# Stick-breaking sums over later keys: fp32r products of a high and a low part in place of fp32 products

## The reference

```
z = einsum('bhqd,bhkd->bhqk', q, k) / sqrt(64)
causal = key_pos < t
log_keep = where(causal, log_sigmoid(-z), 0)
tail = cumsum(log_keep, axis=keys, reverse=True)
between = concatenate([tail[..., 1:], 0])
weights = where(causal, exp(log_sigmoid(z) + between), 0)
out = einsum('bhqk,bhkd->bhqd', weights, v)
...
y = concatenate([y_dilated, y_lru, y_stick * silu(gate)])
x = x + y @ w_out
```

## Time and profile before

| | |
|---|---|
| median of 3 runs | 1189.01 us (1188.92 to 1189.37) |
| profiled execution | 1189.2 us, span 1187.4 us |
| granted TensorE clock | 0.998 of full |
| busy | TensorE 98%, its weight loads 88%, VectorE 62%, ScalarE 48%, GpSimd 2% |
| HBM | 177 GB/s over the span |

### The profile page before, as it was taken

How to read it: one execution, slowest core, us unless ns; L and a number is a source line. 1 busy time by engine, 2 the same in 40 slices (tenths; PEclk the granted TensorE clock), 3 DMA queues, 4 the chain that set the end, 5 groups by cost and what they waited for, 6 DMA issues and landing times.

```text
span 1187.4 us, 18024 instructions
## 1 busy us (share of the span) xinstructions
PE 1164.1 (98%) x7560; PEld 1041.3 (88%) x7560; DVE 737.5 (62%) x982; ACT 570.6 (48%) x656; POOL 25.9 (2%) x35
## 2 busy tenths in 40 slices
PE   6999999999999999999999999999999899999997
PEld 5978998998999988888998898899988689978995
DVE  4866655668555456685755657755554667775674
ACT  5454445534444434444444534445432466855673
POOL 0000000001000000000000000000000100000000
PEclk9999999999999999999999999999999999999999
DMA  8744545555765554644545457565556353437320
GB/s 293 261 168 156 174 146 177 188 194 169 265 191 186 175 197 141 237 153 142 177 142 192 163 194 230 195 211 183 194 196 213 124 193 128 141 128 253 130 84 35
DMA packets 129823, 211.44 MB, mean 178 GB/s; under 512 B 6480, under 2 KB 52560, under 8 KB 129616
## 3 DMA queue, kind: packets, MB, share of 16 engines
q1 hardware_dynamic: 126944, 202.96, 50.9%
q0 software_dynamic: 1744, 6.29, 1.9%
q10 hardware_dynamic: 1056, 1.05, 0.3%
HBM read 209.24 MB, written 1.05 MB: 177 GB/s over the span
## 4 chain that ended last, share of the span: by engine, by line
PE 93%; DVE 3%; ACT 3%; issue 1%; DMA 0%; POOL 0%; DVEq 0%; POOLq 0%; ACTq 0%
PE ps L432 89%; PE ps L621 1%; ACT wh L895 1%; PE ps L656 1%; PE ps L756 0%; DMA hml<-in_xT 0%; PE ps L604 0%; PE ps L563 0%; ACT sg L1058 0%; ACT xh L931 0%; DVE sg L1592 0%; DVE wl L1318 0%; PE ps L628 0%; PE ps L738 0%; DVE yl L1783 0%
## 5 line engine op out<-in xcount | busy, mean ns | idle before, releaser
L1318 DVE TENSOR_TENSOR wl<-raw,wh 128x2048 fp32r<-128x2048 f32 (+2 forms) x195 | 429.0, 2206 | 187.4 <-ACT wh L895 187.0
L895 ACT ACTIVATE wh<-raw 128x2048 fp32r<-128x2048 f32 (+2 forms) x195 | 364.1, 1874 | 180.7 <-PE ps L432 173.2
L432 PE MATMUL ps<-xh,wh 128*128 128x256 f32 (+1 forms) x1200 | 338.3, 282 | 0.0
L432 PE MATMUL ps<-xh,wl 128*128 128x256 f32 (+1 forms) x1200 | 333.0, 277 | 0.0
L432 PE MATMUL ps<-xl,wh 128*128 128x256 f32 (+1 forms) x1200 | 333.0, 277 | 0.0
L432 PEld LDWEIGHTS ps<-xh,wh 128*128 128x128 f32 (+1 forms) x1200 | 224.4, 187 | 3.7 <-issue 2.4
L432 PEld LDWEIGHTS ps<-xl,wh 128*128 128x128 f32 (+1 forms) x1200 | 224.3, 187 | 0.9
L432 PEld LDWEIGHTS ps<-xh,wl 128*128 128x128 f32 (+1 forms) x1200 | 223.9, 187 | 0.4
L432 PE MATMUL ps<-wh,xh 128*128 128x512 f32 (+1 forms) x512 | 204.9, 400 | 13.6 <-DVE wl L1318 11.3
L432 PE MATMUL ps<-wh,xl 128*128 128x512 f32 (+1 forms) x512 | 197.6, 386 | 0.0
L432 PE MATMUL ps<-wl,xh 128*128 128x512 f32 (+1 forms) x512 | 197.6, 386 | 0.0
(11 more groups left out here) (246 smaller groups left out, 1367.2 us busy)
## 6 DMA issues: line engine op xcount, KB each, us to landing
raw<-in_w_in SPq DMA_DIRECT2D x91, 1024.0 KB, 5.0
raw<-in_w_gate_up SPq DMA_DIRECT2D x88, 512.0 KB, 4.8
raw<-in_w_down SPq DMA_DIRECT2D x20, 1024.0 KB, 5.0
raw<-in_w_out SPq DMA_DIRECT2D x16, 1024.0 KB, 4.8
raw<-in_w_proj_ret SPq DMA_DIRECT2D x8, 1024.0 KB, 5.0
raw<-in_w_proj_mlstm SPq DMA_DIRECT2D x8, 1024.0 KB, 4.9
rows<-in_ln_g POOLq DMA_DIRECT2D x4, 512.0 KB, 4.1
rows<-in_ln_b POOLq DMA_DIRECT2D x4, 512.0 KB, 5.9
```

The lines of the kernel that those rows point to most:

```text
L432: return pe.matmul(o, a, b, start=start, stop=False, skip_group_check=True)
L895: act.activation(stretch(wh, u, 0, m), raw[u % RAW][:, 0:m], ACT.Copy).then_inc(s_hi, 1)
L1318: dve.tensor_tensor(stretch(wl, u, a, nk * n), raw[u % RAW][:, a:nk * n], f32(stretch(wh, u, a, nk * n)), ALU.subtract).then_inc(s_lo, 1 i ...
```

## The change

`stick_tail` on VectorE gets more operations. Behind the present one it copies `ee` (f32) to a new fp32r tile `eeh`, and then writes the difference of `ee` and `eeh` as fp32r into `eel`, which has the same place in memory as `ee`. In group 0 it also copies the triangle and the block of ones to the fp32r tiles `below` and `ones`, in every layer. `stick_sums` on TensorE multiplies both parts, in fp32r: per head two products of 256 columns and four of 128, where it had one of 256 and two of 128 in fp32.

```diff
@@ -276,6 +276,12 @@
+        with ExitStack() as areas:
+            sb("pad4", [P, 4096], F32, areas)
+            eel = sb("eel", [P, H, 384], F32R, areas)
+            below, ones = sb("below", [P, P], F32R, areas), sb("ones", [P, P], F32R, areas)
+            sb("pad5", [P, 256], F32, areas)
+            eeh = sb("eeh", [P, H, 384], F32R, areas)
@@ -783,9 +789,12 @@
                 pe.wait_ge(s_tail, 2 * l + g + 1)
                 for h in (2 * g, 2 * g + 1):
                     bank, fill = open_aux(f"2k{h}", l)
-                    mm(bank[:, 0:S], C("ltri"), ee[:, h, 0:S], True)
-                    mm(bank[:, P:S], C("ptri", P, S), ee[:, h, S:S + P], False)
-                    mm(bank[:, S:S + P], C("ltri"), ee[:, h, S:S + P], False).then_inc(fill, 1)
+                    for part in (eeh, eel):
+                        mm(bank[:, 0:S], below[:, :], part[:, h, 0:S], part is eeh)
+                        r = mm(bank[:, S:S + P], below[:, :], part[:, h, S:S + P], False)
+                    for part in (eeh, eel):
+                        r = mm(bank[:, P:S], ones[:, :], part[:, h, S:S + P], False)
+                    r.then_inc(fill, 1)
@@ -1805,7 +1814,13 @@
             def stick_tail(l, g):
                 dve.wait_ge(s_ln, 2 * l + g + 1)
-                dve.scalar_tensor_tensor(out=fe[g], in0=fz[g], scalar=0.0, in1=fe[g], op0=ALU.max, op1=ALU.add).then_inc(s_tail, 1)
+                hi, lo = ([a[:, 2 * g:2 * g + 2, :].rearrange("p h c -> p (h c)") for a in (eeh, eel)])
+                after(own(dve.scalar_tensor_tensor(out=fe[g], in0=fz[g], scalar=0.0, in1=fe[g], op0=ALU.max, op1=ALU.add)))
+                after(own(dve.tensor_copy(hi, fe[g])))
+                if g == 0:
+                    dve.tensor_copy(below[:, :], C("ltri"))
+                    dve.tensor_copy(ones[:, :], C("ptri", P, S))
+                dve.tensor_tensor(lo, fe[g], f32(hi), ALU.subtract).then_inc(s_tail, 1)
```

## The result

The change takes **1191.86 us** (median of 16 runs, 1189.95 to 1193.01) against 1189.68 for the kernel before (16 runs, 1188.89 to 1190.23) beside it on the same chip. The ratio is 1.0017, with a 95% interval of 1.0009 to 1.0025: about 2.0 us slower by the ratio. That lies inside the range of the prediction and near its 2.1.

A forecast was written before the change was run, and what follows sets the result against it. The y chain, not TensorE, was taken to set the time at project, with VectorE 0.36 us from the bound. Head 3's delay, 2 x 1.06 = 2.1 us slower on the median 1189.01, gave 1191.1; range 1189.6 to 1192.2.

The forecast's parts named there:

- The frame: At project in each layer TensorE waits for yl; its earlier savings lengthen waits, chain delays are paid in full per layer.
- The y chain: From the second stick_sums of g 1 through ScalarE's exp, the scan and yh/yl pairs to the last yl; 14 us off TensorE.
- head 3: VectorE's second stick_sums of g 1, where the y chain starts; forecast 1.06 us later per layer through TensorE.
- VectorE's part: Longer tails in stick_tail: g 0 costs nothing, g 1 makes head 3 0.64 us later per layer.
- rival 2: The copy to eeh runs at the two-tensor rate, head 3 1.25 us late; 1191.5 us; chance 0.18.
- The tail of g 0: VectorE's stick_tail operations for group 0, ending at 1022.89 instead of 1021.00, all hidden by a 2.10 us wait for ScalarE.
- the price of a 128-column fp32r product: In TensorE's stick_sums blocks, bounded by 0.115 and 0.22 us, taken as 0.22; a block then costs 2.24 instead of 1.75.
- rival 1: fp32r is cheap at 128 columns too (0.115 to 0.12 us), VectorE's 0.64 per layer decides; 1190.3 us; chance 0.26.
- the row of 4 columns at 0.115: Six TensorE records with only 4 columns take 0.69 us; taken as the lower bound, 0.115, for 128 columns.
- It is 0.36 us early, no more: At head 3 VectorE could have started 0.36 us earlier than it did, the most the chain could gain per layer.
- the 1.06 a layer: Forecast delay of head 3, set by TensorE's slower blocks: 1.06 us per layer, over VectorE's 0.64.

The follow-up runs named there:

- TensorE's part alone: The change with stick_tail writing fp32r in one operation, read by both product rounds, low part left out; 1187.87 us, ratio 0.9989 to the kernel before.
- VectorE's part alone: The change with all its VectorE operations but the fp32 products of the kernel before; 1190.80 us, ratio 1.0013 to the kernel before.
- the later split: The change with one VectorE weight split moved from ahead of the sums of g 1 to behind head 3; 1187.76 us, ratio 0.9989 to the kernel before.

## Why the prediction came out as it did

**The frame was right, the engine that decides in it was not.** The y chain sets the time at `project`, TensorE's gain ahead of it only lengthens its waits, and a delay of head 3 is paid once per layer; but VectorE delays head 3, where the forecast had TensorE. TensorE's part alone, VectorE's part alone and the later split show this from three sides: take the chain's delay away and the kernel is 1.5 us faster, keep it alone and it is 1.45 slower.

**VectorE's part was right.** Head 3 was to be 0.64 late by VectorE, and is by 0.63. The copy to `eeh` was costed at 0.56 and takes 0.56, so rival 2 is out. The Trainium skill, "VectorE: DVE Perf Modes", section "The perf-mode tier table (the rule you actually need)", puts fp32 copies within SBUF one mode above two-tensor operations, at twice the rate. The trace agrees, 0.56 against 0.95 for 768 columns. The tail of g 0 and its two small copies went into the wait for ScalarE, of which 0.24 is left (0.21 was forecast: 1023.10 - 1022.89).

**The step that failed is the price of a 128-column fp32r product.** "I take 0.22": it is 0.11, at the lower bound. The block went from 1.75 to 1.37 and not to 2.24, so TensorE doesn't push head 3, and the delay is VectorE's 0.63 and not 1.06. That is rival 1, which I had given 0.26, and its sum for the chain, 2 x 0.64 = 1.3, stands against 1.24 measured in the two layers. "Nothing shows that the cheap rate of fp32r reaches below 256 columns" was true, but the row of 4 columns at 0.115 was the better guide: what it showed, the cost of a record with next to nothing to stream, is what 128 columns cost too. The 0.22 was the price of an fp32 product, which has two records of 0.11; an fp32r product has one.

**"It is 0.36 us early, no more"** was too small as well. I looked only at VectorE's wait ahead of head 3. The waits ahead of head 0 and head 1 were TensorE's too, and a faster first block gives them back; with TensorE's part alone it came to 0.78. It did not enter the sum.

**What made up the rest was not foreseen.** The chain's 1.24 would have given 1190.9 on 1189.68; the median is 1191.86. The rest goes with TensorE's clock, granted at half behind the wait for `yl` in layer 1. The fall stands in the two profiles of the change that are of the upper group, not in the one of the lower group. The kernel before and the later split, with an early rise too but waits of 0.32 and 0.37, don't have it. And filling the wait with products, with the chain left as it was, removed the two groups and made the kernel about 1 us faster by the medians. So it is luck that the total came near 2.1: of the 1.06 a layer only 0.62 is there, which makes 1.24 us, and 0.8 to 1 us at the median, which stood in no term of the sum, goes with the clock.

**Open:** why layer 1's wait brings the fall and layer 0's, as long (1.71 to 1.73), did in none of the three profiles; what makes one execution's clock rise early and another's late; and whether the three runs of the change with the other order of y that lie 2 us high, at the lower mean clock, have their fall behind the wait of 1.70 us for the norm. None of the three was profiled.

## What to carry to other kernels

Before counting a saving on the busiest engine, find the next place at which it waits for another, and ask what the change adds to that other engine's path; here a gain of 1.5 us on TensorE and a chain 1.2 us later became 2.8 us of waiting, and moving one weight split turned a loss of 2.2 us into a gain of 1.6 (by the medians). Let a product read first what is ready first: the order of four y was worth as much as the whole change cost. And a wait on TensorE that grows beyond what it was can cost a second time, in the clock behind it, so read the granted clock after every wait that a change lengthens, in more than one execution.

## What the hardware showed that I had not expected

- An fp32r product of 128 columns starts 0.11 us after the last, one of 256 columns 0.12, one of 512 columns 0.23; fp32 at 128 columns had cost 0.21. So eight products of 128 columns in fp32r (0.88) replaced four in fp32 (0.84) at next to no cost, and the gain came from the 256-column ones, 0.48 for four where two in fp32 took 0.83.
- TensorE's clock was granted at 0.50 to 0.57 behind a wait of 1.72 us, three products and another wait of 0.22, for over 3 us, about 1.6 us lost. In the change's first profile the same waits, 1.73 and 0.22 long, left it at 1.00, with ten products in the two us where the others have five or six:

```profile
1172.00:1174.00 2.00, 2.00 (x10) 1.64 (x9) 0.00 (x0) 0.00 (x0) 0.00 (x0) 1.00 0.00 0
```

- Where the fall shows goes with the start: all seven executions whose clock came up by 16.3 us had it near 940 us, of the six in which it took until 17.0 or more one had it. The change's three profiles fit that for layer 1 too, two early ones with the fall and a late one without. A single profile shows only one of these kinds.
- Twelve products more, of 0.23 us each, went with a kernel about 1 us faster by the medians.
